# One transformer layer with a routed mixture of experts: latent tiles before context tiles, quartered modulation loads, earlier modulation columns, and a rearranged last attention step

## What is computed

```
mod_x = silu(c) @ w_mod + b_mod          # six rows of 1024: sh1, sc1, g1, sh2, sc2, g2
mod_c = silu(c_ctx) @ w_mod + b_mod
hx = rms_norm(x, g) * (1 + sc1) + sh1    # hc likewise, from ctx with mod_c
f, q, k, v = split(hx @ w_in)            # 256 + 768 + 256 + 256 columns
q, k = rope(heads(q)), rope(heads(k))    # heads of 64, rms-normalised; context keys without rope
attn = softmax(q k^T / 8) v              # 12 query heads, 4 key heads, 1280 keys
four = real(fft2(f)) @ w_four
x = x + g1 * (concat(four, attn) @ w_out)
h2 = rms_norm(x) * (1 + sc2) + sh2
aff = softmax(h2 @ w_router)             # 16 experts; each takes its 128 best tokens
x = x + g2 * sum_e gate_e * swiglu_e(h2[idx_e])
out = rms_norm(x)
```

## Time and profile before

| what | value |
|---|---|
| median of 3 runs | 2044.84 us (2044.82 to 2049.74) |
| profiled execution: its time, its span | 2045.49 us, 2043.6 us |
| TensorE busy | 1855.5 us, 91% of the span |
| VectorE, ScalarE, GpSimd busy | 1610.3, 1304.6, 301.7 us |
| stage A, stage B | 0 to 264.8 us, 264.8 to 881.3 us |
| search for the best tokens, first gather | 883.3 to 920.5 us, to 928.5 us |
| experts, final norm | to about 2012 us, to 2043.6 us |

### The profile page before, as it was taken

How to read it: one execution, slowest core, us unless ns; L and a number is a source line. 1 busy time by engine, 2 the same in 40 slices (tenths; PEclk the granted TensorE clock), 3 DMA queues, 4 the chain that set the end, 5 groups by cost and what they waited for, 6 DMA issues and landing times.

```text
span 2043.6 us, 28018 instructions
## 1 busy us (share of the span) xinstructions
PE 1855.5 (91%) x8691; PEld 1457.8 (71%) x8691; DVE 1610.3 (79%) x2067; ACT 1304.6 (64%) x1921; POOL 301.7 (15%) x295
## 2 busy tenths in 40 slices
PE   6799979999899889717999999999999999999995
PEld 3677746666666666416888888888888888888884
DVE  5578747766766767477989988998899989998996
ACT  3544247666756756425777777777777777777774
POOL 0133221110111111101201100111011101110113
PEclk8999979999999999958999999999999999999998
DMA  8266590210110120028999999999999999999996
GB/s 351 93 186 164 141 242 28 63 38 25 62 44 28 51 62 10 31 103 332 411 386 386 377 391 390 385 375 389 394 386 378 386 391 385 372 390 397 375 373 256
DMA packets 103938, 512.28 MB, mean 251 GB/s; under 512 B 12064, under 2 KB 36040, under 8 KB 53200
## 3 DMA queue, kind: packets, MB, share of 16 engines
q1 hardware_dynamic: 97696, 489.11, 63.4%
q0 software_dynamic: 4752, 17.30, 3.1%
q10 hardware_dynamic: 1440, 5.24, 0.7%
HBM read 481.71 MB, written 27.28 MB: 249 GB/s over the span
## 4 chain that ended last, share of the span: by engine, by line
PE 53%; DVE 2%; DMA 1%; POOL 0%; ACT 0%; issue 0%; DVEq 0%; ACTq 0%; POOLq 0%
PE banks L1564 34%; PE banks L1589 17%; PE banks L1576 1%; PE banks L1545 1%; DVE topi L1423 1%; DVE top L1421 1%; DVE cand L1424 1%; DMA xe<-h_scratch,icol 0%; DVE raw L1519 0%; POOL fst L1337 0%; DMA out<-raw 0%; ACT banks L1411 0%; POOL fst L1335 0%; DVE ysc L1483 0%; DVE ysc L1526 0%
## 5 line engine op out<-in xcount | busy, mean ns | idle before, releaser
L1455 DVE TENSOR_TENSOR w_lo<-raw,w_hi 128x2048 fp32r<-128x2048 f32 x256 | 574.9, 2287 | 67.2 <-ACT w_hi L1363 67.2
L1363 ACT ACTIVATE w_hi<-raw 128x2048 fp32r<-128x2048 f32 x256 | 470.4, 1917 | 8.2 <-DMA raw<-in_w_exp 8.2
L1564 PE MATMUL banks<-w_hi,x_hi 128*128 128x512 f32 x1024 | 405.4, 396 | 1.4 <-DVE x_lo L1449 1.4
L1564 PE MATMUL banks<-w_hi,x_lo 128*128 128x512 f32 x1024 | 399.8, 390 | 0.0
L1564 PE MATMUL banks<-w_lo,x_hi 128*128 128x512 f32 x1024 | 399.3, 390 | 0.0
L1463 DVE TENSOR_TENSOR d_lo<-raw,d_hi 128x1024 fp32r<-128x1024 f32 x256 | 296.2, 1218 | 1.5 <-ACT d_hi L1385 1.4
L1385 ACT ACTIVATE d_hi<-raw 128x1024 fp32r<-128x1024 f32 x256 | 258.1, 1061 | 34.7 <-DMA raw<-in_w_exp 22.1
L1564 PEld LDWEIGHTS banks<-w_hi,x_lo 128*128 128x128 f32 x1024 | 192.6, 188 | 40.8
L1564 PEld LDWEIGHTS banks<-w_hi,x_hi 128*128 128x128 f32 x1024 | 192.9, 188 | 39.7 <-DVE x_lo L1449 1.8
L1038 DVE TENSOR_TENSOR ptl<-banks,pth 128x384 fp32r<-128x384 f32 x320 | 176.5, 555 | 56.3 <-ACT pth L984 52.1
L1564 PEld LDWEIGHTS banks<-w_lo,x_hi 128*128 128x128 f32 x1024 | 193.1, 189 | 38.1
(11 more groups left out here) (210 smaller groups left out, 2751.4 us busy)
## 6 DMA issues: line engine op xcount, KB each, us to landing
raw<-in_w_exp SPq DMA_DIRECT2D x384, 1024.0 KB, 7.9
a_ring<-in_w_mod SPq DMA_DIRECT2D x32, 512.0 KB, 4.7
qt<-q_scratch SPq DMA_DIRECT2D x64, 192.0 KB, 3.6
a_slot<-in_w_mod SPq DMA_DIRECT2D x8, 1024.0 KB, 12.7
a_w_raw<-in_w_in SPq DMA_DIRECT2D x3, 2048.0 KB, 31.3
q_scratch<-a_qst SPq DMA_DIRECT2D x16, 384.0 KB, 3.9
a_xt<-in_x ACTq DMA_DIRECT2D x8, 512.0 KB, 3.3
xr<-in_x SPq DMA_DIRECT2D x8, 512.0 KB, 4.2
```

The lines of the kernel that those rows point to most:

```text
L1363: act.activation(w_hi[which][c][:, :], raw[which][c][:, :], ACT.Copy).then_inc(s["hi_done"], 1)
L1455: dve.tensor_tensor(w_lo[which][c][:, :], raw[which][c][:, :], w_hi[which][c][:, :].bitcast(F32), ALU.subtract).then_inc(s["lo_done"], 1)
L1564: i = pe.matmul(psum[:, 2 * (j % 2) + which, :], x_[par][:, k, :], w_, start=(k == 0 and w_ is hi and x_ is x_hi), stop=(k == KD - 1 and x ...
```

## The change

- **Order of tiles and chunks.** Latent tiles are 0 to 7, context tiles 8 and 9. Chunks are loaded and split in the order 1, 0, 2, and all of them before the loop over tiles. `pairs` and the loads of the Fourier tables move to turn 8, ahead of the last values and stores, and the pair buffers to other addresses.
- **Columns ahead of splits.** VectorE completes the modulation columns before it splits a weight chunk.
- **Quarters of two units.** A ring load brings a quarter of both units (two runs of 2 KB in each partition instead of one of 4 KB); VectorE finishes a load after four operations. The first tile's modulation is done before the first turn, its row product in the second tile.
- **Out-projection in slots.** In steps 1 to 7 the halves are cut into four slots of two k's, one after each part of heads 4 and 5.
- **Last step.** Five of eight k's (0, 1, 2, 6, 7) are multiplied at the end of slots 0 and 1, in banks 0 and 1, once all exponentials are done; three follow in slots 4 and 5. h2 is multiplied and shifted by halves, all on VectorE; its turns use banks 2 and 3; the router's first four k's wait only for the first half's copy.
- **Candidates.** `cand` is cleared at the opening of stage B and filled in the last step's slot 4, but for the last 128 tokens, whose affinities ScalarE writes there directly.

The diff, cut to its core:

```diff
@@ stage A
-    ring = [at(f"a_ring{i}", [P, HALF_UNIT], F32, (120 + 4 * i) * KB) for i in range(RING)]
+    ring = [at(f"a_ring{i}", [P, 2, QUARTER], F32, (120 + 4 * i) * KB) for i in range(RING)]
-    pm = [at(f"f_pm{i}", [P, TH, FW], F32, (96 + 8 * i) * KB) for i in range(2)]
+    pm = [at(f"f_pm{i}", [P, TH, FW], F32, (8 + 4 * i) * KB) for i in range(2)]
-        return n >= TC
+        return n < TL
-        return 2 * (2, 1, 0).index(c)
+        return 2 * (1, 0, 2).index(c)
@@ SyncE
-                u, half = 2 * (i // 4) + i % 2, i // 2 % 2
-                sp.dma_start(ring[i % RING][:, :], w_mod[NC_UNITS + u][:, half * HALF_UNIT:(half + 1) * HALF_UNIT]).then_inc(ring_in[i % RING], 16)
+                u, part = NC_UNITS + 2 * (i // 4), slice(i % 4 * QUARTER, (i % 4 + 1) * QUARTER)
+                sp.dma_start(ring[i % RING][:, :, :], w_mod[u:u + 2, :, part].rearrange("u p n -> p u n")).then_inc(ring_in[i % RING], 16)
-                if n == TS:
+                if n == TL:
                     tables()
-                for i in range(3) if TC <= n < TS else ():
-                    load(4 * (n - TC) + i)
+                for i in range(3) if n < TL else ():
+                    load(4 * n + i)
@@ ScalarE
-            weights(2, 0)
-            weights(2, 1)
+            weights(1, 0)
+            weights(1, 1)
             turn(0, 0)
             turn(0, 1)
             high(0)
             square(1)
             normal(1)
-            weights(1, 0)
-            weights(1, 1)
+            weights(0, 0)
+            weights(0, 1)
+            weights(2, 0)
+            weights(2, 1)
@@ VectorE
+                for q in (2 * half, 2 * half + 1):
+                    i = 4 * n + q
+                    dve.wait_ge(ring_in[i % RING], 16 * (i // RING + 1))
+                    for k in range(2):
+                        for x in range(2):
+                            ins = weigh(acc[:, x, :], ring[i % RING][:, x, k * UM:(k + 1) * UM], c_sig[:, 2 * q + k, 0:1],
+                                        None if q == 0 and k == 0 else last[x], q == 0 and k == 0)
...
-            for half in range(2):
-                weights(2, half)
             dve.wait_ge(s["c_col_done"], 1)
...
-            low(0)
             weights(1, 0)
             weights(1, 1)
+            low(0)
+            weights(0, 0)
+            weights(0, 1)
+            weights(2, 0)
+            weights(2, 1)
             low(1)
+            modulation(0, 0)
+            modulation(0, 1)
             for n in range(1, TS + 2):
-                if n == TS:
+                if n == TL:
                     pairs()
@@ TensorE
                     project(n, 1)
-                    if n + 1 < TS:
-                        turn(n + 1, 0)
+                    if n == 1:
+                        row(0)
+                    turn(n + 1, 0)
                     project(n, 0)
...
-                    row(n - TC)
+                    if n > 0:
+                        row(n)
@@ stage B, ScalarE
+                    if not cur and i == 4:
+                        act.wait_ge(s["cand_zero"], 1)
+                        act.wait_ge(s["misc_free"], misc(t, 0))
+                        act.activation(cand[0:E, :], aff[:, 0:HALF], ACT.Copy).then_inc(s["cand_done"], 1)
+                        act.activation(cand[H2:EH, 0:HALF - P], aff[:, HALF:N - P], ACT.Copy).then_inc(s["cand_done"], 1)
@@ stage B, VectorE
+                        if not cur:
+                            for c in (slice(0, 512), slice(512, D)):
+                                chain(dve.scalar_tensor_tensor(out=h2[:, c], in0=x2[:, c], scalar=st2[:, 2:3], in1=rows[:, SC2, c],
+                                                               op0=ALU.mult, op1=ALU.mult))
+                                dve.tensor_tensor(h2[:, c], h2[:, c], rows[:, SH2, c], ALU.add).then_inc(s["h2b"], 1)
+                            continue
@@ stage B, TensorE
+                def out_part(j, ks_, first, last):
+                    for k in ks_:
+                        ins = pe.matmul(psum[:, bank_of(f"OP{j}", cur), :], mix[:, k, :], wout[:, k, j * 512:(j + 1) * 512],
+                                        start=(first and k == ks_[0]), stop=(last and k == ks_[-1]))
+                    return ins
+                        if prev and cur and i in (4, 5):
+                            j = i - 4
+                            if c == 0:
...
+                                pe.wait_ge(s["mix_done"], 4 * t)
+                                pe.wait_ge(s["ymix_done"], t)
+                                misc_free(f"OP{j}")
+                            ins = out_part(j, (2 * c, 2 * c + 1), c == 0, c == NCH)
+                            if c == NCH:
+                                ins.then_inc(s["misc_mm"], 1)
+                    if not cur and i in (4, 5):
+                        pe.wait_ge(s["mix_done"], 4 * t)
+                        out_part(i - 4, LATE, False, True).then_inc(s["misc_mm"], 1)
+                    if not cur and i in (0, 1):
+                        pe.wait_ge(s["exp_done"], NS * TL)
+                        pe.wait_ge(s["mix_done"], 4 * t - 2)
+                        pe.wait_ge(s["ymix_done"], t)
+                        out_part(i, EARLY, True, False)
@@ stage M
-            act.activation(cand[0:E, :], aff[:, 0:NH2], ACT.Copy).then_inc(s["cand_done"], 1)
-            act.activation(cand[H2:EH, :], aff[:, NH2:N], ACT.Copy).then_inc(s["cand_done"], 1)
```

## The result

The changed kernel takes 2032.32 us (median of 4, 2030.01 to 2035.89) against 2046.41 us of the kernel before on the same chip: a ratio of 0.9927 with an interval of 0.9906 to 0.9947, 14.1 us less. Forecast were 2022.8 us, in a range of 2014 to 2033. It is faster, by two thirds of what I had worked out, and lies at the upper edge of the range.

A forecast was written before the change was run, and what follows sets the result against it. Expert products on TensorE hold half the span but start behind the first stage and attention, so time removed there counts: 13.5 + 2.0 + 6.5 = 22.0 us off 2045.49 gives 2023.5, median 2022.8; range 2014 to 2033, own range 2018 to 2028.

The forecast's parts named there:

- the stalled cycle: Latent tiles: with one quarter awaiting the fourth load, 20.7 to 20.9 us becomes 19.4, so TensorE's 19.63 sets the period.
- the ring stays the gate: Latent tiles: quarters land 1.4 us later, six tiles keep today's length, 8.7 us, giving 2031.5 us; chance 0.18.
- The estimate from the Trainium skill's figure: Ring loads: 128 more runs at about 10.5 ns per packet would add 1.3 us to each landing.
- the row of the 1 KB runs: Ring loads: 384 KB of queries in 384 runs land in 3.9 us, so no landing difference was taken for quarters.
- Head: Start of stage A: columns ahead of weight splits start TensorE's projections at 42.65 instead of 45.60, 2.95 us gained.
- Tail: End of stage A: with context last, little hides the last latent tile's chain; last projection 198.7, attention starts at 251.4.
- two pauses in the context tiles: Stage A's tail: TensorE waits for values before projections 8 and 9, near 5 us each, 4.9 worked out before 8.
- Slots: Attention steps 1 to 7: cut out-projections save TensorE's idle time of 0.29 us, 2.0 us over seven steps.
- the large saving: Attention steps 1 to 7: slots hide more, waits around heads 3 to 6 go, 9.3 instead of 2.0, 2015.5; chance 0.13.
- the rival's price per slot: Attention steps 1 to 7: 56 slots each cost time; from 0.4 us the gain is gone, 0.6 gives 2056; chance 0.05.
- Last step: Last attention step: early out-projection k's, h2 by halves and candidates off the chain save 6.4, rounded to 6.5 us.
- The sum: Whole kernel: 13.5 for the first stage, 2.0 for slots and 6.5 for the last step make 22.0 us.

The follow-up runs named there:

- the refill kept back: Changed kernel, but a tile's first three ring loads wait for the whole accumulation of the tile before: 2028.4 us, ratio 0.9911.
- either order mended: Two runs on the changed kernel: ScalarE's query copy ahead of normalising, 2022.08 us; SyncE's fourth ring load ahead of row store and stores, 2018.45 us.
- with both: Changed kernel with query copy ahead of normalising, fourth ring load ahead of stores, and GpSimd's bias rows moved into attention step 0: 2011.51 us, ratio 0.9810.
- the three later runs that leave stage A's queues alone: Changed kernel with out-projection as blocks in steps 1 to 7, 0.9917; bias rows inside attention step 0, 0.9867; weight splits ahead of columns, 0.9930.
- once the queues were in order: Changed kernel with query copy before normalising, fourth load before stores, bias rows in step 0: 2011.51 us with quarters, 2023.24 us with ring halves.
- the two other runs on that kernel: Kernel before with one edit each: query copy ahead of normalising, ratio 1.0004; fourth ring load ahead of row store and stores, ratio 0.9967.
- that of the halves: Changed kernel with ring loads back to halves of one unit and the old accumulation order: 2035.03 us, ratio 0.9943.
- the kernel with blocks: Changed kernel with the out-projection of attention steps 1 to 7 as two blocks of eight matmuls again: 2033.99 us, ratio 0.9917.

## Why the prediction was right in sign and off in size

**The step that failed** is "the stalled cycle of 20.7 to 20.9 becomes 19.4, which is no longer above TensorE's own 19.63. I take 19.63." It measured 21.8: 19.6 of work, 1.7 of waiting and 0.5 for the slower clock behind the two longest waits. I had seen rightly that the fourth load stood behind the stores and that a quarter less of the accumulation waits for it. I took all else in the tile as fixed, the moment of the stores among it. Freeing the ring earlier lets three loads go out ahead of the next activations, so these land 2.8 us later; ScalarE's order turns that into a late query copy, SyncE's into a late fourth load. The last row product came at 211.75 instead of 198.7, 13 us late, and that is more than the whole error of the sum, 7.9. Four runs bear on it: with the refill kept back 4.3 us of stage A return, with either order mended 9.5 and 12.1, and with both the period is 19.3.

**The rival "the ring stays the gate"** named the right resource with a wrong mechanism. A quarter of 256 runs did not land 1.4 us later but 0.3 (5.0 against 4.7), 0.4 to 0.7 in the three later runs that leave stage A's queues alone, and not at all once the queues were in order (5.5 against 5.5). The estimate from the Trainium skill's figure of about 10.5 ns per packet ("DMA: Bandwidth & Descriptors", section "Bandwidth") would have had 1.3; the skill has that figure from a 4 KB transfer issued from GpSimd. So the row of the 1 KB runs was the better guide. Its 2031.5 us came near the measured time all the same, since a tile of old length was the outcome by another road. It was luck, too, that the time fell into the range: the forecast's own range ended at 2028, and 2032.3 lies in it only because it had been stretched toward this rival.

**Head:** 2.95 us forecast; 3.72 in the profile, of which 0.6 is an earlier landing, so 3.1. The new order of columns brings 1.8 of it. The rest, 1.3, is chance in the profile of before: counted from the last modulation unit, its first projection comes at 18.8 us, those of the two other runs on that kernel at 17.5 and 17.9.

**Tail:** 52.7 us from the last row product to attention, measured 50.3. Its two pauses in the context tiles, 4.9 forecast for the first and 6.8 for the second, are 2.35 and 5.48 us.

**Slots:** 2.0 forecast, 2.4 by the steps of the run that undoes them. The waits for exponentials did not fall (28.1 us after, 27.9 in the earlier trace rows), so neither the large saving nor the rival's price per slot was there.

**Last step:** 6.5 forecast; from the first flush to the search 46.81 us became 39.73, 7.1 less. It is 39.7 to 39.8 in four other profiles and 41.3 to 41.5 in six. The two values differ by one row, the late twelve matmuls of the out-projection, in the profile of after and in that of the halves, and by the granted clock of that stretch, 1.00 and 0.76:

```profile
853.68 5.42 PE L1137 MATMUL banks<-wout,mix 128*128 128x512 f32 x12 [1.71 <-POOL mix L930]
```
```profile
852.41 7.11 PE L1137 MATMUL banks<-wout,mix 128*128 128x512 f32 x12 [1.72 <-POOL mix L930]
```
```profile
853.60:859.10 5.50, 5.42 (x12) 2.20 (x12) 1.39 (x2) 0.00 (x0) 0.03 (x1) 1.00 0.00 0
```
```profile
852.40:859.50 7.10, 7.09 (x12) 2.79 (x12) 1.38 (x2) 0.00 (x0) 0.00 (x0) 0.76 0.00 0
```

The kernel before has the same two forms: its first sixteen matmuls take 7.13 us at a clock of 1.00 in the profile of before, and in the two other runs on it 8.8 us at 0.81, where flush to search is 49.1 and 49.2. So like compared with like the last step gives 7.1 us at the full clock, and 7.7 with the fall.

The chain behind them ran as worked out in the first case. Counted from the first flush (832.57 after, 836.46 before, so 3.9 us are to be added): late products end at 863.0 (863.3 forecast), halves of h2 are ready at 868.1 and 869.5 (868.4 and 869.8), the search starts at 876.2 (876.8). One turn runs beside the other's copy, and the candidates are off the path.

**The sum.** 22.0 forecast. Stage A 2.8, attention 11.4 in a usual profile (618.4 to 607), together 14.2; the medians differ by 14.1. Last step and slots make 9.5 of attention's 11.4. The rest goes with falls of the clock. From the opening to the last step's first flush the profile of before takes 571.6 us, with four of seven steps at 0.98 or 0.99, and the two other runs on that kernel 569.0 and 568.9, like the 568.8 of the kernel with blocks. That the falls are fewer after the change is a matter of these profiles; whether the change makes them fewer is not shown.

## What to carry to other kernels

When a buffer comes free earlier, ask which transfers will now start earlier, which load on another queue they will run beside, and what stands behind that load on the engine that awaits it. Put copies whose input is there ahead of work that waits for a transfer: worth nothing before this change, about 10 us after it. Put loads that gate ahead of stores that wait: 6.6 us before, about 14 after. The two don't add up. A moved step takes its signals with it: moving a 0.3 us fill cost 7 us through a queue that waited for it.

## Not expected of the hardware

- A 512 KB load of activations landed in 3.3 us where the last ring load ahead of it had been issued some 4 us before, and in 6.1 us right behind three ring loads of 512 KB from another queue (medians). With the refill kept back the ring's own landing rose from 5.0 to 6.3 us instead.
- Twice as many runs of half the length (2 KB instead of 4 KB) cost 0.3 to 0.7 us in 4.7, and nothing in 5.5 with the queues in order.
- The same twelve matmuls took 5.42 us in five profiles and 6.9 to 7.1 in six others, after the same idle time of 1.7 us. In the profile of after their granted clock is 1.00, in that of the halves 0.76: there the first five matmuls start 0.8 to 0.9 us apart, the last seven 0.43. What decides whether the clock falls, these runs don't show.
